# First attention of a hybrid layer: value columns made stationary in two halves, row tiles mixed, gates turned before the product

## The reference

```python
h = x @ w_in[l]
(qa, ka, va, ga, iq, ik, iw, c_q, c_kv, k_rope, gb) = _split_cols(h)
o_a = _dsa_branch(qa, ka, va, iq, ik, iw) * jax.nn.silu(ga)   # softmax over the 128 keys an indexer picks, 8 heads x 64
o_b = _mla_branch(c_q, c_kv, k_rope, ...) * jax.nn.silu(gb)   # low rank q and kv, 8 heads, causal
out = jnp.concatenate([o_a, o_b], axis=-1) @ w_out[l]
x = _layernorm(DEEPNORM_ALPHA * x + out, ln_g[l], ln_b[l])
```

## Time and profile before

| | |
|---|---|
| median of 3 runs | 302.06 us (301.6 to 327.76) |
| the profiled execution | 301.67 us, span 299.9 us |
| TensorE busy | 291.2 us, 97% of the span, 1664 matmuls |
| VectorE, ScalarE, GpSimd busy | 228.5, 165.6, 169.8 us (76%, 55%, 57%) |
| chain that ended last | TensorE 93%, VectorE 2%, all others 1% or less |
| of it, first attention's outputs (L1369) | 5% |
| of it, transposes of probabilities (L1353) | 6% |
| mean granted TensorE clock | 0.992 of full speed |

### The profile page before, as it was taken

How to read it: one execution, slowest core, us unless ns; L and a number is a source line. 1 busy time by engine, 2 the same in 40 slices (tenths; PEclk the granted TensorE clock), 3 DMA queues, 4 the chain that set the end, 5 groups by cost and what they waited for, 6 DMA issues and landing times.

```text
span 299.9 us, 5192 instructions
## 1 busy us (share of the span) xinstructions
PE 291.2 (97%) x1664; PEld 248.6 (83%) x1664; DVE 228.5 (76%) x523; ACT 165.6 (55%) x397; POOL 169.8 (57%) x197
## 2 busy tenths in 40 slices
PE   8999999999999999999999999999999999999990
PEld 7999987778888888888888789998677788888890
DVE  2898689879999999994134663564898878977785
ACT  4754533692252272383267787888877786553200
POOL 5798965106999975445317697630594161817211
PEclk9999999999999999999999999999999999999996
DMA  7965552200533723220056577301940000030412
GB/s 230 354 183 179 144 149 75 67 0 0 154 96 102 207 76 105 70 72 0 0 149 143 211 203 156 125 2 43 359 161 3 0 0 2 36 106 3 140 70 72
DMA packets 19547, 31.86 MB, mean 106 GB/s; under 512 B 6496, under 2 KB 9056, under 8 KB 19520
## 3 DMA queue, kind: packets, MB, share of 16 engines
q1 hardware_dynamic: 19088, 31.35, 34.4%
q10 hardware_dynamic: 432, 0.18, 0.3%
HBM read 26.28 MB, written 2.10 MB: 95 GB/s over the span
## 4 chain that ended last, share of the span: by engine, by line
PE 93%; DVE 2%; DMA 1%; ACT 1%; issue 1%; DVEq 0%; ACTq 0%
PE ps L1117 50%; PE ps L1425 15%; PE ps L1353 6%; PE ps L1318 5%; PE ps L1369 5%; PE ps L1384 3%; PE ps L1308 2%; PE ps L1132 2%; PE ps L1311 2%; PE ps L1221 1%; DMA w_raw<-in_w_in 1%; PE ps L1242 1%; PE ps L1398 1%; DVE y_last L1031 0%; ACT probs L684 0%
## 5 line engine op out<-in xcount | busy, mean ns | idle before, releaser
L474 POOL TENSOR_TENSOR w_lo<-w_raw,w_hi 128x512 fp32r<-128x512 f32 (+3 forms) x62 | 79.3, 1301 | 34.0 <-ACT w_hi L573 33.8
L1117 PE MATMUL ps<-w_hi,x_lo 128*128 128x512 f32 (+2 forms) x224 | 82.6, 372 | 0.0
L1117 PE MATMUL ps<-w_lo,x_hi 128*128 128x512 f32 (+2 forms) x224 | 82.5, 371 | 0.0
L573 ACT ACTIVATE w_hi<-w_raw 128x512 fp32r<-128x512 f32 (+3 forms) x62 | 35.9, 590 | 68.9 <-PE ps L1117 61.8
L1117 PE MATMUL ps<-w_hi,x_hi 128*128 128x512 f32 (+1 forms) x188 | 73.6, 391 | 0.0
L1117 PEld LDWEIGHTS ps<-w_hi,x_lo 128*128 128x128 f32 x224 | 42.1, 188 | 6.5
L1117 PEld LDWEIGHTS ps<-w_lo,x_hi 128*128 128x128 f32 x224 | 42.2, 188 | 6.0
L1425 PE MATMUL ps<-wo_hi,oT 128*128 128x512 f32 (+1 forms) x144 | 43.5, 372 | 0.0
L1117 PEld LDWEIGHTS ps<-w_hi,x_hi 128*128 128x128 f32 x188 | 35.3, 188 | 7.1 <-ACT w_hi L573 0.7
L684 ACT ACTIVATE probs<-probs,small 128x512 f32<-128x512 f32 (+3 forms) x64 | 35.8, 559 | 7.6 <-DVE small L944 7.0
L1353 PE MATMUL ps<-ident,probs 128*128 128x128 f32 x160 | 28.3, 274 | 0.4 <-ACT probs L684 0.2
(11 more groups left out here) (164 smaller groups left out, 548.5 us busy)
## 6 DMA issues: line engine op xcount, KB each, us to landing
w_raw<-in_w_in SPq DMA_DIRECT2D x20, 512.0 KB, 3.7
kaT_swap<-kaT SPq DMA_DIRECT2D x8, 256.0 KB, 3.7
w_raw<-in_w_out SPq DMA_DIRECT2D x4, 512.0 KB, 4.9
wo_early<-in_w_out SPq DMA_DIRECT2D x4, 512.0 KB, 5.3
wo_raw_b<-in_w_out SPq DMA_DIRECT2D x4, 512.0 KB, 5.6
x_res<-in_x SPq DMA_DIRECT2D x4, 512.0 KB, 6.6
x_raw<-in_xT SPq DMA_DIRECT2D x3, 512.0 KB, 6.9
out_y<-y SPq DMA_DIRECT2D x6, 256.0 KB, 2.1
```

Of the source, the lines that this page charges most:

```text
L474: pool.tensor_tensor(w_lo[:, s, 0:n], w_raw[:, s, 0:n], w_hi[:, s, 0:n], ALU.subtract).then_inc(w_lo_ready, 1)
L573: act.activation(dst, w_raw[:, s, 0:n], ACT.Copy).then_inc(w_hi_ready, 1)
L1117: ins = mm(dst, a, b, start=start and j == 0, stop=stop and j == len(pairs) - 1)
```

## The change

Names of lines here are of before where nothing else is said.

- **Order of units.** The 32 units of the first attention come in two blocks of 16: row tiles 3 and 0, then 2 and 1. In a block two heads of the longer tile alternate with the same two heads of the shorter one.
- **Outputs.** Instead of after each unit, they are issued every fourth iteration for four units. The values (128 x 64) are stationary, and the transposed probabilities (128 columns) stream. Heads 2n and 2n + 1 write to partitions 0 to 63 and 64 to 127 of the same columns, so each uses one half of the array's columns, and their products alternate. The result comes out transposed already. Block 1 uses the banks ps_o, block 2 the banks ps_y.
- **Buffers.** Seven buffers of transposed probabilities are in use at a time; in the second block two of the seven are other ones, which wait for a transfer out of their place.
- **Copies.** VectorE copies the transposed probabilities of three units in four, ScalarE those of every fourth.
- **Gates.** GpSimd scales the gates of a tile by the reciprocal sums (`scale_gate_a`), TensorE transposes them (iterations 28, 36, 38, 30 for tiles 3, 2, 1, 0), ScalarE copies them at once into the gates' own place (`turn_gate`), and VectorE multiplies the output banks by them (`gate_oaT`). `normalise` and `apply_gate` are gone. ScalarE makes the high part from there at unit 33, GpSimd the low part of tile 3.
- **Output projection.** The first half of tile 3 is issued three products a unit in units 41 to 48. GpSimd makes three of the low weight splits among its merges.

```diff
+    BLOCKS = [(0, 3), (1, 2)]
+    BLOCK_UNITS = 2 * HEADS
     def unit(u):
-        v, h = divmod(u, HEADS)
+        if u < NU_A:
+            n, r = divmod(u, BLOCK_UNITS)
+            v, h = BLOCKS[n][r % 4 // 2], r // 4 * 2 + r % 2
+        else:
+            v, h = divmod(u, HEADS)
+    def buffer_of(u):
+        r = u % BLOCK_UNITS % 7
+        return r if r < 5 else r + 2 * (u // BLOCK_UNITS)
-    o_norm = sb("o_norm", 92, [P, A_WIDTH])
-    probsT = sb("probsT", 26, [P, 3, BANK])
+    probsT = [sb(f"probsT{j}", kib, [P, BANK]) for j, kib in enumerate((24, 26, 28, 30, 92, 88, 90, 94, 96))]
+        def by_dve(u):
+            return u < NU_A and u % 4 != ACT_COPY
+        def copy_free(eng, u):
+            if u < NU_A:
+                if last_user(u) is not None:
+                    eng.wait_ge(pv_done, last_user(u) + 1)
+                elif buffer_of(u) >= 7:
+                    eng.wait_ge(qpe_placed, 16 * P // SQ)
+                return probsT[buffer_of(u)][:, 0:unit(u)[3]]
...
+            def scale_gate_a(v):
+                m = ORDER[v]
+                pool.wait_ge(rinv_a_ready, A_RANK.index(v) // 2 + 1)
+                wait_tok(pool, G_GA, m)
...
+            def turn_gate(v):
+                n = slot_of[v, 0]
+                act.wait_ge(transposed, n + 1)
+                act.activation(gate[:, ORDER[v], 0:A_WIDTH], ps_pT[:, n % 2], ACT.Copy).then_inc(gate_a_turned, 1)
...
+            def copy_probsT(u):
+                dve.wait_ge(transposed, slot_of[u] + 1)
+                V.tensor_copy(copy_free(dve, u), ps_pT[:, slot_of[u] % 2, 0:unit(u)[3]]).then_inc(probsT_copied_dve, 1)
+            def gate_oaT(v):
+                half = gate[:, ORDER[v], 0:A_WIDTH]
+                dve.wait_ge(gate_a_turned, A_RANK.index(v) + 1)
+                dve.wait_ge(pv_done, BLOCK_UNITS * (A_RANK.index(v) // 2 + 1))
+                V.tensor_tensor(half, oa_bank(v), half, ALU.mult).then_inc(o_ps_read, 1)
...
             def outputs(u):
                 v, m, h, N = unit(u)
                 if v < TT:
-                    pe.wait_ge(probsT_copied, u + 1)
-                    for j in range(m + 1):
-                        ins = mm(ps_o[:, v % 2, h * A_DIM:(h + 1) * A_DIM], probsT[:, u % 3, j * P:(j + 1) * P],
-                                 va[:, j, h * A_DIM:(h + 1) * A_DIM], start=(j == 0), stop=(j == m))
-                    ins.then_inc(pv_done, 1)
+                    if u % 4 < 3:
+                        return
+                    for w in (u - 3, u - 1):
+                        v, m, h, N = unit(w)
+                        for a in range(2):
+                            wait_copied(pe, w + a)
+                        for j in range(m + 1):
+                            for a in range(2):
+                                ins = mm(oa_bank(v)[A_DIM * a:A_DIM * (a + 1), h // 2 * P:(h // 2 + 1) * P],
+                                         va[:, j, (h + a) * A_DIM:(h + a + 1) * A_DIM],
+                                         probsT[buffer_of(w + a)][:, j * P:(j + 1) * P], start=(j == 0), stop=(j == m))
+                                if j == m:
+                                    ins.then_inc(pv_done, 1)
...
-                if 0 <= u - A_HALF_AT < 12:
-                    out_products(0, 2 * (u - A_HALF_AT), 2 * (u - A_HALF_AT + 1))
+                if 0 <= u - A_HALF_AT < 8:
+                    out_products(0, 3 * (u - A_HALF_AT), 3 * (u - A_HALF_AT + 1))
...
-O_FIRST = 16
-A_HALF_AT = 34
+O_FIRST = 33
+TURN_AT = [26, 34, 36, 28]
+ACT_COPY = 3
+VB_EARLY = 22
+A_HALF_AT = 41
 POOL_PAIRS = 1
-VB_EARLY = 20
```

More of the change, by code:

```diff
@@ L319, in out_ps, with wait_copied, oaT, oa_bank @@
             return bank[:, 0:PIECES[i][b].stop - PIECES[i][b].start]
+        def by_dve(u):
+            return u < NU_A and u % 4 != ACT_COPY
+        def wait_copied(eng, u):
+            n = sum(by_dve(w) for w in range(u + 1))
+            if by_dve(u):
+                eng.wait_ge(probsT_copied_dve, n)
+            else:
+                eng.wait_ge(probsT_copied, u + 1 - n)
+        def copy_free(eng, u):
[5 more added lines that the diff above has]
+                return probsT[buffer_of(u)][:, 0:unit(u)[3]]
+            if u >= NU_A + 3:
+                eng.wait_ge(pv_done, u - 2)
+            return probsT_b[:, u % 3, 0, 0:unit(u)[3]]
+        def oaT(i):
+            return gate[:, ORDER[i], 0:A_WIDTH].rearrange("p (a b) -> p a b", a=4)
+        def oa_bank(v):
+            return (ps_o, ps_y)[A_RANK.index(v) // 2][:, A_RANK.index(v) % 2]
         def pair_done(g):
@@ L712, in copy_oT_hi @@
                 if b == 0:
-                    act.wait_ge(transposed, n + 1)
-                    src = ps_pT[:, n % 2].rearrange("p (a b) -> p a b", a=4)
+                    act.wait_ge(o_ps_read, A_RANK.index(i) + 1)
+                    src = oaT(i)
                 else:
@@ L739, in _ @@
             for u in range(NU + T_LAG):
-                if u >= T_LAG:
+                if u >= T_LAG and not by_dve(u - T_LAG):
                     copy_probsT(u - T_LAG)
@@ L1050, in _ @@
                     mask_unit(u)
+                if u >= T_LAG and by_dve(u - T_LAG):
+                    copy_probsT(u - T_LAG)
                 if u - T_LAG >= NU_A:
@@ L1057, in _ @@
                 i = v - TT
[L1058 to L1065, removed]
+                if u in (BLOCK_UNITS + 2, NU_A + 2):
+                    row_sums_a(u // BLOCK_UNITS - 1)
+                if u - T_LAG - 1 in TURN_AT:
+                    gate_oaT(TURN_AT.index(u - T_LAG - 1))
                 if v > TT and j == 2:
@@ L1393, in o_transposes @@
                 if b == 0:
-                    pe.wait_ge(o_ready, i + 1)
+                    pe.wait_ge(gate_a_scaled, A_RANK.index(i) + 1)
                 else:
@@ L1452, in _ @@
             out_products(TT - 2, done, NSTEP - LAST_STEPS)
-            for b in range(2):
-                o_transposes(TT - 1, b)
+            o_transposes(TT - 1, 1)
             out_products(TT - 2, NSTEP - LAST_STEPS, NSTEP)
```

106 lines of the change are left out of this document (59 added, 47 removed).

## The result

The changed kernel took 306.59 us (median of four runs, 304.92 to 306.74), the one before 302.12 beside it: a ratio of 1.0141, 95% interval 1.0095 to 1.0187. Measured once more on another occasion it took 305.01 (304.79 to 305.61), ratio 1.0102, interval 1.0084 to 1.0119. So it is 1 to 1.4% slower. The profiled execution was one of 306.74 us, with a span of 304.9 against 299.9.

The account below looks back on a forecast made before the run. TensorE was taken to bound the first attention, with halved outputs paid back as waiting for long units. 301.67 us profiled + 2.1 to unit 36 + 0.5 + 0.4 behind it = 304.7; forecast 304.6, range 298 to 313.5.

Parts of the forecast that it names:

- The burst: First attention: outputs of four units in a row take 1.07 us plus 0.3 for switching, 1.37 us; bounds 1.07 and 2.44.
- The overlap of halves: In each burst, upper and lower column halves run side by side, so twenty records take 1.07 us instead of 2.14.
- The exposed latency: First attention: 2.43 us from long scores to transposes no longer covered; groups of four units take 5.16 and 4.72 us.
- The sign to look for: In the changed trace: TensorE idle 0.9 us before a group's first long transposes, 0.5 in the second half.
- The extras of the first attention: Added to its groups: query transposes +0.4, unit 16's copy +1.0, ScalarE's copy of the first turned gates +0.4 us.
- Unit 16's copy: Mid first attention: VectorE's copy waits for buffer 0 until iteration 19's burst, holding up masks 19 and 20: +1.0 us.
- The turn: Passage into the second attention: units 32 to 36 +0.4 us; behind them +0.5 for products and gate transpositions, +0.4 for VectorE.
- has room: GpSimd, busy 19.69 of 34.21 us, then 1.17 of 6.44, takes four gate scalings and moved weight splits at no cost.
- Removed work: Normalising and gating leave VectorE; nobody had waited for them, and copies take the same room: nothing gained or lost.
- TensorE's own work sets the pace: Rival: in the first attention masks and Exps keep ahead, groups cost 3.95 and 3.91 us, 294 to 298 us; chance 0.20.
- the halves don't overlap: Rival: each burst costs 2.44 us, 8.6 us more in all, 313.2 us; chance 0.22.
- VectorE becomes the bound: Rival: VectorE, taking 24 of 32 copies, sets the groups at 3.9 us; no separate time, chance within the first rival.

Follow-up runs that it names:

- e1_burst_early: The changed kernel with each burst of outputs issued one iteration earlier, ahead of the first long unit's transposes: 300.37 us, ratio 0.9947 to the kernel before.
- e7_one_key_tile: The changed kernel with the first attention's outputs multiplying only the first key tile, the other products left out: 300.63 us.
- e5_gate_first: The changed kernel with GpSimd's gate scalings of tiles 2 and 1 moved ahead of the low part of tile 3's outputs: 304.64 us.

## Why the prediction was right, step by step

The forecast was 304.6 us for no measurable change, the result 306.59 and 305.01; the range held both. The kernel is slower by 1.4% and 1.0%, clear of the noise but under the 2% that I had set as the bound; the sum itself, 304.6 against a median of 302.06, had said 0.8%.

- **The burst** of 1.37 us: 1.15 for the records, 1.24 in the chain, and the first long scores behind it 0.43 there for 0.29 in the earlier trace rows, 1.38 in all: right to a tenth. The overlap of halves, which I gave 3 in 4, holds. The 2.38x that I took from the Trainium skill (TensorE: Matmul & The Clock Gate, Part 3) is for three column tiles, and I did not show how it leads to 1.37; two gave 1.95x here, 2.24 us to 1.15.
- **The exposed latency**: 2.43 us forecast, 2.46 measured; groups of 5.16 and 4.72 forecast, 5.13 and 4.67 measured where nothing else stands in them. This was the step that decided the sign, and e1_burst_early (the wait filled) and e7_one_key_tile (the burst shortened) showed it from both sides. The sign to look for came otherwise than I wrote: TensorE idled 0.50 us and not 0.9 before the transposes, because the short scores had waited for a mask too, until 187.87, just behind its reading (187.73 and 0.08). I had left that wait out; the transposes were not ready earlier, so it cost nothing.
- **The extras of the first attention**: 1.8 forecast; the seven groups of the undisturbed execution took 36.83 us for 36.2. The second group was 6.03 where 5.6 was the sum: two query transposes and a long copy stand in the chain, not one. Unit 16's copy cost 0.9 for 1.0. The last group was 5.75 for 5.12 (4.72 and 0.4): behind ScalarE's copy of the gates (0.49) a long copy of VectorE (0.48) stands in the chain too.
- **The clock** was not in the sum. It is 1.4 us of the first measurement. I forecast waits of 0.9 us a group on an engine that had had none, and gave the clock no term for them; the range was wide enough to hold it, by luck.
- **The turn**: +0.4 to unit 36 forecast, +0.23 measured. Behind it +0.9 forecast, +0.78 measured, but with a wrong reason: I charged VectorE with 0.4, and it was GpSimd (0.43 by e5_gate_first), whose moves I had put down as free ("has room"). Room on average is not an early place in its queue: the scaling was third behind a piece that waits.
- **Removed work**: normalising and gating were to be free before. No run puts them back; the sums above come out without a term for them.
- The rival *TensorE's own work sets the pace* is nearer the truth with the burst one iteration earlier (300.37), though above its 294 to 298. The rival *the halves don't overlap* (313.2) is what the kernel with one half measured, 312.9. *VectorE becomes the bound* was dismissed as no separate case; it was none here, but is the next bound once the wait is covered.

## What to carry to other kernels

Work that is made cheaper on the engine that everything waits for may also have been the cover of a latency: before shortening or regrouping it, sum what that engine still does between a unit's request and its use of the answer, and compare it with the latency read from the trace (here 1.5 against 2.4 us). If it falls short, put the grouped work into that gap rather than behind it: the same instructions, one iteration earlier, were worth 4.6 us. And look for a queue's order, not its idle share, when small pieces are moved to it.

## What the runs showed of the hardware

- Two fp32 products with 64 stationary columns each, to the upper and lower half of the output partitions, start 7 ns apart, and such pairs follow each other every 109 ns; twenty records of 128 streamed columns take 1.15 us in pairs and 2.24 in one half.
- With eight records of one half ahead of eight of the other, the burst (1.64 us) was still 0.6 us shorter than in one half. Its starts form two rows of 109 ns steps, from 0 to 0.82 us and from 0.49 us on. Records of different halves therefore need not be neighbours in the program to overlap, and some start ahead of records that stand before them.
- Here the trace goes against the rule of the Trainium skill that the prediction weighed (TensorE: Matmul & The Clock Gate, Part 3: weight loads overlap running matmuls only when the row groups differ). The twenty loads of 64 columns, all on the same rows, lay within the burst and added nothing; and the earlier trace rows spoke against it already, with loads busy 32.50 and matmuls 33.97 of 34.21 us, nearly all of them on all 128 rows. The same part of the page also lets the loads of a background weight buffer go ahead, which the prediction left out. The loads of the burst:

```profile
185.10 1.07 PEld L1459 LDWEIGHTS ps<-probsT,va 128*64 128x64 f32 x20 [0.17 <-DVE probsT L1044]
```

- The same program with the same light stretch (TensorE busy 2.54 of 4.0 us, no idle stretch over 0.61 us) fell to the 1.2 GHz level for 3.4 us in one profiled execution and not in another.
